# A bidirectional SSD scan's second pass: step widths moved into the exponent, both directions' decays added before one product, running sums spread by bf16 picks

## The chip, the cores and the metric

One NeuronCore of a Trainium2 chip runs the whole program. The metric is the time of one launch on the device in microseconds (us). Below, PE is TensorE, DVE is VectorE, ACT is ScalarE, POOL is GpSimd, and SP is the engine that issues most of the DMAs.

## What is computed

One encoder layer over 2560 tokens of 1024 channels (2048 of one sequence and 512 of another): RMSNorm, an input projection, neighbourhood attention and a bidirectional Mamba-2 scan side by side, an output projection, and a SwiGLU feed-forward part. The change touches the scan (8 heads of 64 channels, state of 128, 2 groups of 4 heads, chunks of 128 tokens). Cut to what matters:

```python
dt = softplus(dt_raw + dt_bias);  A = -exp(A_log)        # per direction
a_cs = cumsum(dt * A)                                    # inside a chunk of 128
Lmat = exp(where(tril, a_cs[l] - a_cs[s], -inf))
y_diag = ((C @ B.T) * Lmat) @ (x * dt)
states = B.T @ (exp(a_cs[-1] - a_cs) * x * dt)           # one per chunk
y_off  = exp(a_cs) * (C @ h_prev)                        # h_prev = h * exp(a_cs[-1]) + states
y = y_forward + y_backward + D_skip * x
g = rmsnorm_by_group(y * silu(z)) * ssm_norm_w
```

The backward direction is the same over the flipped sequence.

## The kernel before, in words

The program is a row of phases with a barrier of all engines between them: `in_proj_phase`, `attention_phase`, `ssd_phase`, `out_proj_phase`, `ffn_up_phase`, `ffn_down_phase`. Only `ssd_phase` (from L1198) is changed, and the inputs that feed it. Each engine's program is written out by hand, in order, with semaphores between engines; tiles are doubled by the chunk's parity (`par`), and loops run over 10 pairs of the 20 chunks.

Set-up (L1350 to L1389): the step widths `dt` of both directions are turned to tokens by partition, put through softplus on DVE with exponentials from ACT, and a table `tab` is filled with 16 columns each (8 heads, 2 directions) for `A_` (dt·A), `NB` (minus the running sum forward, plus the exclusive one backward), `E_` (the decay for the state's share), `DT` (dt), `CD` (a chunk's decay) and `W_` (a token's weight in the state). PE makes the running sums by products with triangles (`upper`, L1457).

First pass (to L1481), from the last chunk to the first. The helper `ahead` puts each engine one chunk ahead. PE turns x and B to tokens by partition (`turn`, L1466, L1468) and makes both directions' states (`states`, L1479). ACT copies x, B and the forward states out of PSUM (L1426, L1428, L1432). DVE copies a piece of the table (L1393), weighs x twice (`xw`, L1398) and adds the backward state `h_b` (L1406). POOL makes `h_cut`, the state times the chunk's decay (L1445). SP loads `xc` per chunk (L1326).

Second pass (L1484 to L1852), from the first chunk on. Each engine runs `step(now, after, later, before)`: it finishes chunk `now`, prepares chunk `after`, and writes out chunk `before`. In words, per step:

- PE: `across` (C times the two states, L1820, L1823), `prefixes` 0, `products` (C·B, L1779), `prefixes` 1, `diagonal` 0, `prefixes` 2, `diagonal` 1, `prefixes` 3, `turn` (L1832). A quarter q is a direction (q % 2) of a group (q // 2). `prefixes` lays a mask in PSUM by one bf16 product (L1788) and adds for each of 4 heads the running sums along the columns: the weights are one table column spread over 128 columns, the moving operand a triangle, both f32 (L1792). `diagonal` multiplies the decays by `xdt`, forward and backward into one accumulation (L1807, L1808).
- ACT: copies C·B out (`cb`, L1739), takes the exponentials of quarters 0 and 1 with the `NB` column as bias (L1744), then squares, logarithm and root of the group norm of `before` (L1751 to L1756), then quarters 2 and 3.
- DVE: `across` (L1634, L1636 from PSUM, L1639 adds the forward state `h_f`), `mix` 0 (decay times `cb`, L1625), `norm` (L1660), `mix` 2, `outputs` (L1646, L1649, L1654), `table` (copy L1616 and x·dt forward L1618), `out_turned` (L1666).
- POOL: `h_cut` (L1711), `skip` (L1715), x·dt backward (L1697), skip + off_b (L1721), `mix` 1 and 3 (L1703).
- SP: loads of B/C and z, stores of the result.

The two lines of the PE part that the change replaces:

```python
last = pe.matmul(ps_r[q % 2][:, h], tab_c[:, par, at:at + 1].broadcast_to([P, P]), upper[:, d],
                 start=False, stop=h == GH - 1)
```

## Time and profile before

| what | value |
|---|---|
| median of 3 runs | 3426.62 us (3421.67 to 3434.69) |
| the profiled execution | 3428.72 us, span of its instructions 3426.6 us |
| share of the span that PE, DVE, ACT, POOL are busy | 94%, 59%, 41%, 21% |
| granted TensorE clock, mean | 0.972 |
| scan set-up and first pass | about 1191 to 1286 us of the span |
| second pass | about 1286 to 1519 us |

The profile is one execution. A row of the timeline gives an instruction's start and duration and, in brackets, how long its engine had been idle and what released it. PE is PE's matrix products, PEld its weight loads, which overlap them; an f32 product shows as two instructions. A step of 1 in a slice's clock is 2.4 GHz.

### The profile page before, as it was taken

Reading aid. Unit: us, or ns where it says so; the run is one execution under the profiler, and the core shown is the slowest. Engines: PE = TensorE matmul, PEld = TensorE weight load, DVE = VectorE, ACT = ScalarE, POOL = GpSimd, SP = SyncE. Lnnn points to the kernel's source line nnn. Section 1 sums busy time; section 2 is a strip of 40 time slices with the busy share of each in tenths; the row PEclk is TensorE's granted clock in tenths of the full one; section 3 lists DMA queues with packets and bytes.
Section 4 is the critical chain, followed back from the end, with each engine's and each line's share of the span. In section 5 each row is a group of like instructions: output and inputs, shape, how many; then the busy total and the mean of one; then the engine's idle time right before and its main releaser. Section 6 shows DMA issues by size and latency. Waiting matters only on the chain. (4 is left out here: it accounts for less than half of the span.)

```text
span 3426.6 us, 48500 instructions
## 1 busy us (share of the span) xinstructions
PE 3205.6 (94%) x16456; PEld 2762.9 (81%) x16456; DVE 2031.9 (59%) x3070; ACT 1390.9 (41%) x2610; POOL 720.0 (21%) x683
## 2 busy tenths in 40 slices
PE   7999999996999779979979999999999998999999
PEld 6877777774777558968858999999999997887887
DVE  3446556473666578974447555755576665555655
ACT  3333434354667535542214333433343333434443
POOL 5453534412333236742220000000000000000000
PEclk9999999998999989989989999999999999999999
DMA  8686858567433032236656454745475555666776
GB/s 267 232 292 219 327 179 330 201 232 132 87 83 75 29 86 68 66 128 197 204 183 229 148 162 150 235 151 159 150 227 175 174 174 201 215 220 236 272 248 214
DMA packets 458415, 630.02 MB, mean 184 GB/s; under 512 B 133120, under 2 KB 271920, under 8 KB 453856
## 3 DMA queue, kind: packets, MB, share of 16 engines
q1 hardware_dynamic: 431808, 522.36, 48.0%
q0 software_dynamic: 23600, 100.80, 8.4%
q10 hardware_dynamic: 2880, 5.24, 0.4%
q8 instruction: 71, 1.16, 0.1%
q14 instruction: 56, 0.46, 0.0%
HBM read 451.25 MB, written 177.75 MB: 184 GB/s over the span
## 5 line engine op out<-in xcount | busy, mean ns | idle before, releaser
L65 PE MATMUL u_acc<-u_h_hi,u_w_hi 128*128 128x448 f32 (+1 forms) x1848 | 657.5, 356 | 23.9 <-DVE u_h_lo L2333 21.4
L66 PE MATMUL u_acc<-u_h_lo,u_w_hi 128*128 128x448 f32 (+1 forms) x1848 | 656.9, 355 | 0.0
L67 PE MATMUL u_acc<-u_h_hi,u_w_lo 128*128 128x448 f32 (+1 forms) x1848 | 656.8, 355 | 0.0
L65 PEld LDWEIGHTS u_acc<-u_h_hi,u_w_hi 128*128 128x128 f32 x1848 | 348.0, 188 | 44.3 <-issue 22.9
L67 PEld LDWEIGHTS u_acc<-u_h_hi,u_w_lo 128*128 128x128 f32 x1848 | 347.9, 188 | 18.5
L66 PEld LDWEIGHTS u_acc<-u_h_lo,u_w_hi 128*128 128x128 f32 x1848 | 348.0, 188 | 18.3
L2577 ACT CAST d_hi<-d_raw 128x896 fp32r<-128x896 f32 (+1 forms) x231 | 225.0, 983 | 279.4 <-PE d_acc L67 140.9
L460 DVE TENSOR_TENSOR i_w_lo<-i_raw,i_w_hi 128x2048 fp32r<-128x2048 f32 x60 | 158.0, 2633 | 295.7 <-ACT i_w_hi L332 295.7
L65 PE MATMUL d_acc<-d_hi 128*128 128x512 f32 x770 | 302.0, 392 | 17.2 <-DVE d_lo L2598 13.0
L2598 DVE TENSOR_TENSOR d_lo<-d_raw,d_hi 128x896 fp32r<-128x896 f32 (+1 forms) x231 | 252.0, 1132 | 111.1 <-ACT d_hi L2577 105.7
L66 PE MATMUL d_acc<-d_lo,d_hi 128*128 128x512 f32 x770 | 301.4, 391 | 0.0
L67 PE MATMUL d_acc<-d_hi,d_lo 128*128 128x512 f32 x770 | 301.3, 391 | 0.0
L65 PE MATMUL i_acc<-i_w_hi,i_h_hi 128*128 128x512 f32 x640 | 258.6, 404 | 15.3 <-DVE i_ev L524 15.3
L66 PE MATMUL i_acc<-i_w_lo,i_h_hi 128*128 128x512 f32 x640 | 256.7, 401 | 0.0
L67 PE MATMUL i_acc<-i_w_hi,i_h_lo 128*128 128x512 f32 x640 | 256.3, 400 | 0.0
L2276 ACT ACTIVATE u_gate<-u_gate 128x448 f32<-128x448 f32 (+1 forms) x99 | 55.8, 563 | 402.7 <-DVE u_gate L2376 206.3
L2321 DVE TENSOR_TENSOR u_w_lo<-u_w_lo,u_w_hi 128x512 fp32r<-128x512 f32 x264 | 180.6, 685 | 50.9 <-ACT u_w_hi L2261 43.5
L65 PEld LDWEIGHTS d_acc<-d_hi 128*128 128x128 f32 x770 | 145.6, 189 | 48.6 <-DVE d_lo L2598 13.3
L1164 PE MATMUL a_ps_o<-a_probT,a_v 128*64 128x128 f32 x1024 | 147.9, 283 | 34.8 <-ACT a_probT L1066 19.6
L1164 PEld LDWEIGHTS a_ps_o<-a_probT,a_v 128*64 128x64 f32 x1024 | 109.0, 138 | 85.8 <-ACT a_probT L1066 49.7
L332 ACT CAST i_w_hi<-i_raw 128x2048 fp32r<-128x2048 f32 x60 | 114.6, 1910 | 144.8 <-PE i_acc L67 140.0
L964 DVE CUSTOM_DVE_ANT_1 a_prob<-a_ps_s,a_bias 128x384 f32<-128x384 f32 (+2 forms) x160 | 93.4, 584 | 132.7 <-PE a_ps_s L1144 130.3
(256 smaller groups left out, 6411.4 us busy)
## 6 DMA issues: line engine op xcount, KB each, us to landing
u_w_lo<-w_ops SPq DMA_DIRECT2D x264, 256.0 KB, 2.9
i_raw<-w_in_dram SPq DMA_DIRECT2D x60, 1024.0 KB, 6.8
u_w_raw<-w_ffn_dram SPq DMA_DIRECT2D x198, 256.0 KB, 3.1
d_raw<-wd_ops SPq DMA_DIRECT2D x132, 256.0 KB, 5.7
d_raw<-hid_ops SPq DMA_DIRECT2D x154, 192.0 KB, 6.1
d_raw<-w_down_dram SPq DMA_DIRECT2D x99, 256.0 KB, 5.7
i_ops<-w_ffn_dram POOLq DMA_DIRECT2D x44, 512.0 KB, 6.3
w_ops<-i_ops POOLq DMA_DIRECT2D x22, 1024.0 KB, 6.9
```

The costliest lines, as they stand in the source:

```text
L65: pe.matmul(out, w_hi, x_hi, start=first, stop=False, skip_group_check=resumed)
L66: pe.matmul(out, w_hi, x_lo, start=False, stop=False, skip_group_check=resumed)
L67: return pe.matmul(out, w_lo, x_hi, start=False, stop=last, skip_group_check=resumed)
L332: act.copy(w_hi[:, par], raw[:, par]).then_inc(slot_hi_done[par], 1)
L460: dve.tensor_tensor(w_lo[:, par], raw[:, par], w_hi[:, par].bitcast(F32), ALU.subtract) \
L964: dve.tensor_tensor_reduce(prob[:, a % 4, 0:n].rearrange("p (r c) -> p r c", c=32), ps_s[a % 2][:, 0:n].rearrange("p (r c) -> p r c", c=32 ...
L1164: last = pe.matmul(ps_o[HEAD * par:HEAD * (par + 1), c], v[:, par, c * KG + FIRST[b] + j], probT[:, a % 2, j], start=j == 0, stop=j == COU ...
L2276: act.activation(gate[:, c, 0:n], gate[:, c, 0:n], ACT.Silu).then_inc(silu_done, 1)
L2321: dve.tensor_tensor(w_lo[:, n], weights(n), w_hi[:, n].bitcast(F32), ALU.subtract) \
L2577: act.copy(hi[:, r, 0:TB + w], raw[:, r, 0:TB + w]).then_inc(hi_done, 1)
L2598: dve.tensor_tensor(lo[:, r, 0:TB + w], raw[:, r, 0:TB + w], hi[:, r, 0:TB + w].bitcast(F32), ALU.subtract) \
```

## The change

It does the following.

- The bias column `NB` gets ln(dt) added (dt held at 1.2e-38 or more), so that the exponentials carry the step width. The weighed copies `xdt` (L1618 on DVE, L1697 on POOL) go, and `diagonal` takes `x_tok` itself.
- With one x for both directions, a group's two decays are added first and multiplied by `cb` once: DVE for group 0, POOL for group 1, instead of two products on each. `diagonal` then has 4 products a group instead of 8.
- The running sums are no longer made by PE for each head in the second pass. The first pass makes them once per chunk: POOL copies the chunk's `A_` columns (`a_now`), PE multiplies by the triangles (two f32 products of 16 rows), and the sums are split into three bf16 parts, high (ACT), rest (DVE), middle (ACT), low (POOL). At the end SP moves middle and low beside high, 48 rows in all. The second pass spreads a head's row by a bf16 product with constant 0/1 weights (`picks`, 48 rows).
- The second pass's table copy and the norm's two multiplies go from DVE to ACT.

The diff, cut to its core ("..." marks what is left out):

```diff
@@ first pass, set-up
+                    link(dve.tensor_scalar(na, cols(DT), SMALLEST, None, ALU.max))
+                    dve.sem_inc(dt_made, 1)
...
-                    link(dve.tensor_scalar(cols(NB, 0), half(pf, 0), -1.0, None, ALU.mult))
-                    link(dve.tensor_copy(cols(NB, 1), half(px, 1)))
+                    dve.wait_ge(log_made, 1)
+                    link(dve.scalar_tensor_tensor(cols(NB, 0), half(pf, 0), -1.0, half(na, 0), ALU.mult, ALU.add))
+                    link(dve.tensor_tensor(cols(NB, 1), half(px, 1), half(na, 1), ALU.add))
...
+                    act.activation(na, na, ACT.Ln).then_inc(log_made, 1)
@@ first pass, per chunk
+                        dve.tensor_tensor(sum_rest[:, par], ps_b[par][0:H2, KB], sums_bf[0:H2, bass.ds(c * P, P)],
+                                          ALU.subtract).then_inc(sum_rest_done[par], 1)
...
+                        act.copy(sums_bf[0:H2, bass.ds(c * P, P)], ps_b[par][0:H2, KB]).then_inc(sum_high_done[par], 1)
...
+                        act.wait_ge(sum_rest_done[par], i + 1)
+                        act.copy(sum_mid[:, bass.ds(c * P, P)], sum_rest[:, par]).then_inc(sum_mid_done[par], 1)
...
+                    def next_a(i, par, c):
+                        if not isinstance(i, int) or i > 0:
+                            pool.wait_ge(x_turned[par], i)
+                        pool.tensor_copy(a_now[:, par].unsqueeze(2), a_f_b[:, :, at(c)]).then_inc(a_ready[par], 1)
...
+                            pool.wait_ge(sum_mid_done[par], i + 1)
+                            pool.tensor_tensor(sum_low[:, bass.ds((c - par) * P, P)], sum_rest[:, par],
+                                               sum_mid[:, bass.ds((c - par) * P, P)], ALU.subtract).then_inc(sum_low_done[par], 1)
...
+                        pe.wait_ge(a_ready[par], i + 1)
+                        pe.wait_ge(sum_high_done[par], i)
+                        pe.wait_ge(sum_rest_done[par], i)
...
+                        for d in range(2):
+                            last = pe.matmul(ps_b[par][0:H2, KB], a_now[:, par, d], upper[:, d], start=d == 0, stop=d == 1)
...
+                    sp.dma_start(picks[:], pick).then_inc(picks_loaded, 16)
...
+                    sp.dma_start(sums_bf[H2:2 * H2], sum_mid[:]).then_inc(sums_moved, 16)
+                    sp.dma_start(sums_bf[2 * H2:3 * H2], sum_low[:]).then_inc(sums_moved, 16)
+                    sp.wait_ge(sums_moved, 32)
@@ second pass, DVE (POOL the same with 2, 3 and group 1)
-                    def mix(i, par, q):
...
+                        dve.wait_ge(e_done[0], c + 1)
+                        dve.wait_ge(e_done[1], c + 1)
+                        dve.tensor_tensor(decay[:, par, 0], decay[:, par, 0], decay[:, par, 1], ALU.add).then_inc(added[0], 1)
...
                     def step(now, after, later, before):
                         across(*now)
                         if after:
-                            mix(*after, 0)
-                        if before:
-                            norm(*before)
-                        if after:
-                            mix(*after, 2)
+                            mix(*after)
                         outputs(*now)
-                        if later:
-                            table(*later)
                         if before:
                             out_turned(*before)
@@ second pass, ACT
+                                act.wait_ge(cutf_done[par], i)
+                                if not isinstance(c, int) or c > 1:
+                                    act.wait_ge(off_read, c - 1)
+                                act.copy(tab_c[:, par:par + 1], tab[:, bass.ds(c, 1), 0:NTAB]).then_inc(tab_done, 1)
...
+                        act.wait_ge(rstd_done[par], i + 1)
+                        for g in range(GROUPS):
+                            c = slice(g * GW, (g + 1) * GW)
+                            act.activation(g_t[:, par, c], g_t[:, par, c], ACT.Copy, scale=rstd[:, par, g:g + 1]) \
+                               .then_inc(normed[par], 1)
@@ second pass, PE
-                            at = A_ + d * HEADS + g * GH + h
-                            last = pe.matmul(ps_r[q % 2][:, h], tab_c[:, par, at:at + 1].broadcast_to([P, P]), upper[:, d],
+                            last = pe.matmul(ps_r[q % 2][:, h], picks[:, d * HEADS + g * GH + h], sums_bf[:, bass.ds(c * P, P)],
                                              start=False, stop=h == GH - 1)
...
-                            pe.matmul(ps_y[par][:, cols], decay[:, par, 2 * g, h], xdt[:, par, 0, cols], start=True, stop=False)
-                            last = pe.matmul(ps_y[par][:, cols], decay[:, par, 2 * g + 1, h], xdt[:, par, 1, cols],
-                                             start=False, stop=True)
+                            last = pe.matmul(ps_y[par][:, cols], decay[:, par, 2 * g, h], flat2(x_tok[:, bass.ds(c, 1), cols]),
+                                             start=True, stop=True)
```

How the engines' instructions stand now. First DVE in the second pass's loop, even chunk; the rows with `s2_xdt` are the weighing, `s2_decay` the mixing. Before:

```order
L1634 TENSOR_TENSOR s2_off_f<-s2_ps_off0,s2_tab_c 128x512
L1636 TENSOR_TENSOR s2_off_b<-s2_ps_off1,s2_tab_c 128x512
L1639 ISA
L1639 TENSOR_TENSOR s_h_f<-s2_h_cut,s_s_f 128x512
L1623 REGISTER_ALU
L1625 TENSOR_TENSOR s2_decay<-s2_decay,s2_cb 128x512
L1660 TENSOR_SCALAR s2_g_t<-s2_g_t,s2_rstd 128x256 x2
L1625 TENSOR_TENSOR s2_decay<-s2_decay,s2_cb 128x512
L1646 TENSOR_TENSOR s2_off_f<-s2_ps_y0,s2_off_f 128x512
L1649 TENSOR_TENSOR s2_off_f<-s2_off_f,s2_skip 128x512
```

After, the same place:

```order
L1700 TENSOR_TENSOR s2_off_f<-s2_ps_off0,s2_tab_c 128x512
L1702 TENSOR_TENSOR s2_off_b<-s2_ps_off1,s2_tab_c 128x512
L1705 ISA
L1705 TENSOR_TENSOR s_h_f<-s2_h_cut,s_s_f 128x512
L1686 REGISTER_ALU
L1688 TENSOR_TENSOR s2_decay<-s2_decay 128x512
L1691 TENSOR_TENSOR s2_decay<-s2_decay,s2_cb 128x512
L1712 TENSOR_TENSOR s2_off_f<-s2_ps_y0,s2_off_f 128x512
L1715 TENSOR_TENSOR s2_off_f<-s2_off_f,s2_skip 128x512
```

The norm has left the queue, and what follows the add is one product. The norm and the table copy stand on ACT now, in the loop's odd chunk:

```order
L1782 COPY s2_tab_c<-s_tab 128x72
L1783 REGISTER_ALU
L1784 COPY s2_cb<-s2_ps_cb 128x256
L1790 ACTIVATE s2_decay<-s2_ps_r0,s2_tab_c 128x128 x4
L1790 ACTIVATE s2_decay<-s2_ps_r1,s2_tab_c 128x128 x4
L1797 ACTIVATE s2_junk,s2_ss<-s2_g_t 128x256 x2
L1800 ACTIVATE s2_ss_ln<-s2_ss,s_eps 128x2
L1802 ACTIVATE s2_rstd<-s2_ss_ln 128x2
L1806 ACTIVATE s2_g_t<-s2_g_t,s2_rstd 128x256 x2
```

Quarters 2 and 3 of the exponentials come behind L1806. On POOL, in the first pass's loop, a small copy (`a_now`, for the chunk after the next) stands ahead of each h_cut and a subtraction of 16 rows behind it, where h_cut stood alone:

```order
L1506 TENSOR_TENSOR s1_h_cut<-s_h_b,s1_tab_c 128x512
L1509 ISA
L1509 TENSOR_TENSOR s1_sum_low<-s1_sum_rest,s1_sum_mid 16x128
L1491 ISA
L1491 COPY s1_a_now<-s1_a_f_b 128x32
L1506 ISA
L1506 TENSOR_TENSOR s1_h_cut<-s_h_b,s1_tab_c 128x512
```

The next chunk's `a_now` copy is thus queued behind this chunk's subtraction.

## Rows read from the trace of the kernel before

**Rows 1.** The page's busy time, share of the span, instructions, by engine.

```profile
PE 3205.6 (94%) x16456; PEld 2762.9 (81%) x16456; DVE 2031.9 (59%) x3070; ACT 1390.9 (41%) x2610; POOL 720.0 (21%) x683
```

**Rows 2.** Stretches: length, busy time by engine, PE clock, DMA share, GB/s.

```profile
1222.00:1286.00 64.00, 55.74 (x280) 45.28 (x280) 54.54 (x80) 28.95 (x60) 28.28 (x20) 0.94 0.39 111
1286.00:1298.00 12.00, 8.42 (x45) 7.76 (x46) 3.98 (x6) 5.80 (x17) 2.81 (x2) 0.72 0.27 89
...
1384.90:1406.95 22.05, 21.13 (x170) 20.05 (x169) 20.76 (x27) 12.02 (x47) 16.59 (x12) 1.00 0.25 71
```

**Rows 3.** Timeline, PE in one chunk of the second pass: start, us, what.

```profile
1398.34 0.10 PEld L1788 LDWEIGHTS s_ps_r<-s_masks,s_ident_bf 128*128 128x128 bf16 x1 [1.32 <-DVE s_tab_c L1616]
...
1399.35 0.53 PEld L1779 LDWEIGHTS s_ps_cb<-s_bc 128*128 128x128 f32 x4
1399.80 0.10 PEld L1788 LDWEIGHTS s_ps_r<-s_masks,s_ident_bf 128*128 128x128 bf16 x1
...
1399.91 0.38 PE L1788 MATMUL s_ps_r<-s_masks,s_ident_bf 128*128 128x512 bf16 x1
...
1400.12 1.05 PE L1792 MATMUL s_ps_r<-s_upper,s_tab_c 128*128 128x128 f32 x8
...
1400.91 0.30 PEld L1807 LDWEIGHTS s_ps_y<-s_xdt,s_decay 128*128 128x128 f32 x2
...
1402.64 0.15 PEld L1788 LDWEIGHTS s_ps_r<-s_masks,s_ident_bf 128*128 128x128 bf16 x1
...
1406.58 0.47 PEld L1832 LDWEIGHTS s_ps_t<-s_ident,s_g_t 128*128 128x128 f32 x4
1407.02 0.73 PEld L1820 LDWEIGHTS s_ps_off<-s_h_f,s_bc 128*128 128x128 f32 x4
...
1408.64 0.10 PEld L1788 LDWEIGHTS s_ps_r<-s_masks,s_ident_bf 128*128 128x128 bf16 x1
```

**Rows 4.** Timeline, DVE and POOL in the second pass.

```profile
1385.92 0.19 DVE L1616 COPY s_tab_c<-s_tab 128x72 f32 x1
...
1389.69 1.49 POOL L1697 TENSOR_TENSOR s_xdt<-s_x_tok,s_tab_c 128x512 f32<-128x512 f32 x1
...
1390.20 1.52 DVE L1625 TENSOR_TENSOR s_decay<-s_decay,s_cb 128x512 f32<-128x512 f32 x1
...
1394.19 0.68 DVE L1625 TENSOR_TENSOR s_decay<-s_decay,s_cb 128x512 f32<-128x512 f32 x1
...
1408.02 0.19 DVE L1616 COPY s_tab_c<-s_tab 128x72 f32 x1
```

**Rows 5.** Timeline, products and ACT; group norm of the last chunk.

```profile
1498.28 0.53 PEld L1779 LDWEIGHTS s_ps_cb<-s_bc 128*128 128x128 f32 x4
...
1499.09 0.37 ACT L1739 COPY s_cb<-s_ps_cb 128x256 f32<-128x256 f32 x1 [2.63 <-PE s_ps_cb L1779]
...
1499.36 2.18 ACT L1744 ACTIVATE s_decay<-s_ps_r,s_tab_c 128x128 f32<-128x128 f32 x8
...
1514.75 0.42 ACT L1751 ACTIVATE s_junk<-s_g_t 128x256 f32<-128x256 f32 x1 [5.79 <-DVE s_g_t L1654]
...
1516.02 0.20 ACT L1756 ACTIVATE s_rstd<-s_ss_ln 128x2 f32<-128x2 f32 x1
```

**Rows 6.** Timeline, DVE and POOL in the first pass.

```profile
1248.38 2.14 DVE L1398 TENSOR_TENSOR s_xw<-s_x_tok,s_tab_c 128x512 f32<-128x512 f32 x2
1248.41 1.56 POOL L1445 TENSOR_TENSOR s_h_cut<-s_h_b,s_tab_c 128x512 f32<-128x512 f32 x1 [1.41 <-DVE s_h_b L1406]
...
1251.35 2.14 DVE L1398 TENSOR_TENSOR s_xw<-s_x_tok,s_tab_c 128x512 f32<-128x512 f32 x2
```

**Rows 7.** POOL groups by form to 1300 us: count, busy us, mean ns.

```profile
L906 POOL TENSOR_TENSOR a_prob<-a_prob,a_inv 128x512 f32<-128x512 f32 x32 | 33.3, 1042 | 79.1 <-DVE a_inv L979 79.1
...
L906 POOL TENSOR_TENSOR a_prob<-a_prob,a_inv 128x256 f32<-128x256 f32 x16 | 9.8, 614 | 57.0 <-DVE a_inv L979 57.0
```

**Rows 8.** DMA issues of the scan: count, KB each, median us to landing.

```profile
s_bc<-xcT SPq DMA_DIRECT2D x20, 256.0 KB, 3.2
```

More of the change, by code:

```diff
@@ L1264, in ssd_phase @@
             h_cut = sb1("h_cut", [P, 2, D_SSM])
+            a_f_b = sb1("a_f_b", [P, 2, NCH, H2])
+            a_now = sb1("a_now", [P, 2, 2, H2])
+            sum_rest = sb1("sum_rest", [H2, 2, P])
+            sum_mid = sb1("sum_mid", [H2, T], BF16)
+            sum_low = sb1("sum_low", [H2, T], BF16)
             ps_x = [ps1(f"ps_x{i}", [P, KX, P]) for i in range(2)]
@@ L1532, in ssd_phase @@
             e_done = four("e_done")
-            m_done = four("m_done")
+            added = two("added")
+            m_done = two("m_done")
             cb_out = two("cb_out")
@@ L1654, in outputs @@
                         dve.tensor_tensor(g_t[:, par], off_f[:, par], z_t[:, par], ALU.mult).then_inc(gated[par], 1)
-                    def norm(i, par):
-                        dve.wait_ge(rstd_done[par], i + 1)
-                        for g in range(GROUPS):
-                            c = slice(g * GW, (g + 1) * GW)
-                            dve.tensor_scalar(g_t[:, par, c], g_t[:, par, c], rstd[:, par, g:g + 1], None, ALU.mult) \
-                               .then_inc(normed[par], 1)
                     def out_turned(i, par):
@@ L1722, in step @@
                         if after:
[L1723 to L1728 removed]
+                            mix(*after)
+                    mix(0, 0)
                     steps(pool, step)
```

113 lines of the change are left out of this document (64 added, 49 removed).

## Prediction

> **What bounds the kernel now.** I read the page first: TensorE (PE) is busy 94% of the span [rows 1], but that is a mean over phases, and the change touches one phase only, the two scan passes, 327 us of 3427. So I went to the stretches [rows 2]: the first pass takes 64 us for 20 chunks, and in a pair of chunks of the second pass (22.05 us) PE is busy for 21.1 and DVE for 20.8, while ACT has 12.0 and POOL 16.6. Two engines are full there. Then the timeline of PE's weight loads in one chunk [rows 3], where the distance between starts is what a piece really costs. I name them: across (A, four f32 products of 256 columns) 1.62 us, a prefix block (r, one bf16 mask product and four f32 products) 1.11, the C·B products (P) 0.45, a half of the diagonal (D, 8 f32 products) 1.73, the turn (T) 0.44. One chunk is A + 4r + P + 2D + T = 10.4 us. Once a pair PE also sits 1.32 us for DVE's table copy (first of rows 3). The copy recurs after 1408.02 - 1385.92 = 22.10 us [rows 4]: 11.05 us a chunk, and DVE sets it as much as PE.
>
> What DVE spends is partly not its own. Its mix product started at 1390.20 and took 1.52 us, though it is 0.68 where POOL is idle (1394.19); POOL's weighing of x had started at 1389.69 [rows 4]. In the first pass two DVE products of about that length take 2.14 when POOL's h_cut starts 0.03 us behind the first: 0.65, then POOL's piece of some 0.9, then the second 0.6, which is the end of both rows [rows 6]. So operations of DVE with both inputs in SBUF and operations of POOL take turns, about 0.6 us and 1.0 us each.
>
> **Second pass: PE.** The prefix block loses its f32 products for bf16 ones. The mask product, 512 columns in bf16, is followed by the next after 0.21 us [rows 3], so 128 columns are 0.055 by its rate; the bounds are 0.055 and the 0.11 at which f32 passes follow each other (8 in 1.00). I take 0.06: r = 0.11 + 0.22 + 4 x 0.06 = 0.5 with some rounding up (at 0.11 it is 0.66). The Trainium skill ("TensorE: Matmul & The Clock Gate", LDWEIGHTS) puts a weight load at its columns over 1.2 in ns, 107 for 128 columns however few its rows; by that picks would follow at the 0.11 bound, r would be 0.66 and the ring below 8.1 instead of 7.9, still under what I take for the chunk. D has half the products: 0.87, and with a register instruction ahead of each at most 1.3. One chunk is then 1.62 + 4 x 0.5 + 0.45 + 2 x 0.87 + 0.44 = 6.3 us, 7.7 with both upper bounds. PE stops being the bound.
>
> **Second pass: the ring over ACT and PE.** ACT takes over the table copy and the two normalising multiplies, in its in-order queue between quarters 0, 1 and 2, 3 of the decays. PE's turn waits for the multiplies, PE's across, prefix 0 and products stand behind the turn, ACT's cb copy waits for the products, the exponentials stand behind that, the group norm behind them. Once round, per chunk: T 0.49 with its wait, A 1.62, r0 0.5 [rows 3]; products to cb copy 1499.09 - 1498.28 = 0.81, cb to the first exponential 0.27, eight exponentials 2.18 less the last one's tail, 2.0, squares to rstd 1.47 [rows 5]; two multiplies of 256 columns 0.7 (0.42 is such a square, the second overlaps). With one wait of 0.05 that is **7.9 us**. Before, the multiplies were DVE's and PE's queue hid all of this. The moved table copy (0.19 on DVE, about 0.2 on ACT) runs while ACT waits for the products; if that cover goes it costs 0.2 a chunk. The exponent now carries ln dt; that is free there.
>
> **Second pass: the port pair.** DVE loses the table copy, the dt product and the norm; its two mix products become an add and a product. With two SBUF inputs remain h_f, add, product, + skip, gate: 5 x 0.6 = 3.0 us. POOL loses the weighing and keeps five: h_cut, skip, + off_b, add, product: 5 x 1.0 = 5.0. Together 8.0 us, and DVE's other four (from PSUM, 0.6 each, 2.4) run beside POOL. That is just above the ring's 7.9. The turns do not pack: POOL's add waits for quarter 3, and while DVE reads y from PSUM (0.6) POOL is often out of work. I take **8.4 us** a chunk; the floor is 7.9 (ring), the ceiling 9.2 (8.0 + the 0.6 of y + 0.6 of waits between turns). The Trainium skill ("SBUF — State Buffer", Who interferes with whom) states this as an exclusive lock held for a whole instruction. If it were a sharing of bandwidth instead, the ring alone would decide, 7.9; rows 4 and 6 speak for turns.
>
> Saving: 19 chunk periods x (11.05 - 8.4) = **-50.4 us**. The head of the second pass runs at the lower clock (0.72 in 1286 to 1298 [rows 2]) and its first prefixes shorten by about 1 us each: -2 (0 to -3).
>
> **First pass.** DVE is full: period 1251.35 - 1248.38 = 2.97 us [rows 6]. Each chunk gains a subtraction of 128 columns (DVE; between the 0.19 of a 72-column copy [rows 4] and 0.65 of 512 columns: 0.25), two ACT copies of 16 rows (ACT has 1.3 us free), two f32 products on PE (0.43; PE has 0.5 free), and on POOL sum_low and the copy a_now. POOL's 256 columns take 0.61 and its 512 take 1.04 [rows 7], so by a straight line 0.40 and 0.24. The DVE term alone gives 3.22. But POOL is in order, and a ring closes over two chunks: h_b ends, h_cut (0.3 wait, 1.5), sum_low behind DVE's second weighing (to +3.4 us), a_now (+3.65), the two products and their end (+4.4), ACT's copy of x (+5.1), both weighings (+7.2), the subtraction, h_b: 7.3 us for two, 3.65 each. I take 3.64: 19 x 0.67 = **+12.7 us**. Bounds 3.22 (+4.8) and 3.9 (+17.7, each small POOL operation 0.25 dearer over two chunks). Small POOL operations are in no row of this phase, so the ring could be wrong by more than that.
>
> At the end SP moves two 16-row tensors inside SBUF and waits for them, with every engine behind it at the block's end: between an issue alone, 0.4, and that with the landing of a bc load of 256 KB, 3.2 [rows 8], so 3.6. These move 80 KB each; nearer the upper row, I take **+3.0**. The load of picks is issued while the last chunks run and is hidden; if not, at most its own landing, 3. The set-up chain gains a max and a Ln, both under the running-sum products (3.6 us of PE there), and POOL's parts copy, hidden behind DVE's table work: +0.5 for two operations that become two-input ones.
>
> **Sum** against the profiled execution, 3428.7 us (its span is 3426.6): -50.4 - 2 + 12.7 + 3.0 + 0.5 = -36.2, 3392.5. The median of the runs shown is 2.1 lower, so I forecast **3390 us**, 1.1% less. All later phases start earlier and are otherwise unchanged.
>
> **Rivals.**
> *The ring alone decides* (turns pack perfectly, first pass pays only DVE's 0.25): 19 x (11.05 - 7.9) = 59.9; -59.9 - 2 + 4.8 + 3.5 = -53.6, 3373. For it: POOL and DVE already interleave well in rows 4. Against: 8.0 of turns is more than 7.9. Chance 0.20.
> *DVE and POOL do not pack*, 9.2 a chunk: 19 x 1.85 = 35.2; -35.2 - 2 + 12.7 + 3.5 = -21, 3406. For it: POOL would be in work 5.5 of 9.2, and both engines wait for each other three times a chunk (h_cut, off_b, skip). Chance 0.22.
> *The first pass loses more*: the POOL ring at 4.5 us, +29 instead of +12.7, with 8.4 behind it: 3406 too. It means that small POOL operations cost twice the straight line. Chance 0.05.
> *Slower: the clock falls.* PE goes from 21.1 busy of 22.05 to 6.3 of 8.4 a chunk, with a wait of a microsecond or more in each. Rows 2 show the granted clock at 0.72 where PE had stood idle for the bc load, and 1.2 GHz is its lower level. If the whole second pass ran there, PE's 6.3 would be 12.6 us a chunk: 19 x 1.55 = +29, and with the first pass +46: 3472. It costs more than it saves once more than about six tenths of the pass are at the lower level. The Trainium skill's page on TensorE and its clock gate says that idle stretches bring the clock down, which speaks against this change. Against it: the first pass, with PE waiting in every chunk (busy 55.7 of 64), had 0.94 granted including its start [rows 2]. Chance 0.03.
>
> **Numbers.** Forecast (8.2 to 8.7 a chunk) 0.50; the five cases are 0.50, 0.20, 0.22, 0.05, 0.03. A measurement of this kernel can tell about 0.5%, 17 us, from no change. Faster by more needs under 3409.5: the forecast, the ring alone, most of the other two: 0.87. Within 0.5%: 0.09. Slower 0.04. The range holds the first three cases and some of the bounds: 3370 to 3411. The forecast's own is 3383 to 3399.
>
> **What would show it.** Right: a chunk of the second pass recurs every 8.2 to 8.7 us; PE's gap stands ahead of the products or the diagonal, not ahead of prefix 0 for a DVE copy; bf16 picks at about 0.06 us; ACT idle only for the cb copy; DVE's add or product over 1 us when POOL runs. First pass: x copies every 3.6 us, PE's a_now products released by POOL, and about 3 us between the last h_b and the first bc load. Wrong: a period at or under 8.0 (no turns), POOL idle over 3 us a chunk (the ring is longer than I have it), a granted clock under 0.9 in the second pass, or a first-pass period above 4.

## The result, and the profile after

The changed kernel takes 3406.48 us (median of 11 executions, 3391.67 to 3423.13) against 3426.62 of the kernel before (median of the 11 timed beside it): a ratio of 0.9938, with an interval of 0.9917 to 0.9959, so 14 to 28 us less. The forecast was 3390. The profiled execution took 3394.09 us, 34.6 less than the profiled one of before. So there are two questions: whether the 34.6 came from where they were forecast, and why the median has only 20 of them.

The page's busy line of the changed kernel, against [rows 1]:

```profile
PE 3157.7 (93%) x15896; PEld 2674.9 (79%) x15896; DVE 1968.5 (58%) x3011; ACT 1410.6 (42%) x2711; POOL 703.6 (21%) x706
```

It says little: PE does 48 us less, and the span is 34 shorter. The stretches say more. First pass, the gap between the passes, and 30 us of the second pass (length; busy time of PE, PEld, DVE, ACT, POOL; granted clock, DMA share, GB/s), against [rows 2]:

```profile
1217.00:1294.00 77.00, 68.70 (x360) 49.74 (x358) 43.34 (x99) 35.57 (x100) 42.76 (x59) 0.97 0.33 94
1294.00:1306.00 12.00, 4.56 (x20) 2.29 (x20) 0.20 (x1) 4.21 (x12) 0.00 (x0) 0.62 0.38 102
1380.00:1410.00 30.00, 25.95 (x187) 18.96 (x186) 29.09 (x34) 24.92 (x95) 25.01 (x19) 1.00 0.29 86
```

PE is no longer full in the second pass; DVE is in work for 97% of it. The chunk recurs every 8.47 and 8.55 us by turns, where it took 11.05. These rows, of one chunk, are the ring that the forecast described, from one group norm to the next (ACT and PE, in order of time):

```profile
1399.24 0.48 ACT L1797 ACTIVATE s_junk<-s_g_t 128x256 f32<-128x256 f32 x1
...
1400.80 0.91 ACT L1806 ACTIVATE s_g_t<-s_g_t,s_rstd 128x256 f32<-128x256 f32 x2
...
1401.83 0.42 PEld L1876 LDWEIGHTS s_ps_t<-s_ident,s_g_t 128*128 128x128 f32 x4 [1.28 <-issue]
1402.22 0.73 PEld L1864 LDWEIGHTS s_ps_off<-s_h_f,s_bc 128*128 128x128 f32 x4
...
1403.84 0.10 PEld L1837 LDWEIGHTS s_ps_r<-s_masks,s_ident_bf 128*128 128x128 bf16 x1
1404.36 0.22 PEld L1840 LDWEIGHTS s_ps_r<-s_sums_bf,s_picks 48*128 48x128 bf16 x4 [0.42 <-issue]
1404.69 0.52 PEld L1830 LDWEIGHTS s_ps_cb<-s_bc 128*128 128x128 f32 x4
...
1405.44 0.37 ACT L1784 COPY s_cb<-s_ps_cb 128x256 f32<-128x256 f32 x1 [1.53 <-PE s_ps_cb L1830]
1405.70 2.18 ACT L1790 ACTIVATE s_decay<-s_ps_r,s_tab_c 128x128 f32<-128x128 f32 x8
...
1407.71 0.48 ACT L1797 ACTIVATE s_junk<-s_g_t 128x256 f32<-128x256 f32 x1
```

Squares to multiplies 1.56, to PE's turn 1.03, turn 0.39, across 1.62, prefix 0 0.85, products to the cb copy 0.75, to the exponentials 0.26, these 2.01: 8.47 us, the period itself. ACT's idle 1.53 ahead of the cb copy is no reserve, for what it waits for stands behind its own multiplies. The picks' products follow one another after 0.056 us, as forecast, but the block of prefix 0 is 0.85 long and the others are 0.65 to 0.74, not 0.5. The idle 0.42 ("issue") is that of the weight loads between the mask's and the first pick's; part of it is the mask product itself, as the products show:

```profile
1404.05 0.38 PE L1837 MATMUL s_ps_r<-s_masks,s_ident_bf 128*128 128x512 bf16 x1
1404.37 0.39 PE L1840 MATMUL s_ps_r<-s_sums_bf,s_picks 48*128 x4
```

The picks start 0.32 us behind the mask product, where an f32 product of before stood 0.21 behind it [rows 3]: 0.1 us is new there.

The other candidate, the turns of DVE and POOL, in the same chunk:

```profile
1400.83 1.59 POOL L1765 TENSOR_TENSOR s_skip<-s_skip,s_off_b 128x512 f32<-128x512 f32 x1
1401.22 1.75 DVE L1688 TENSOR_TENSOR s_decay<-s_decay 128x512 f32<-128x512 f32 x1
1403.01 0.69 DVE L1691 TENSOR_TENSOR s_decay<-s_decay,s_cb 128x512 f32<-128x512 f32 x1
```

DVE's addition takes 1.75 behind POOL's, and the product after it, with POOL idle, 0.69. Turns are there as forecast; both candidates lie near 8.5, and only runs can tell which decides.

The first pass went from 2.97 to 3.75 us a chunk (forecast 3.64). Its rows, for [rows 6]:

```profile
1244.38 0.58 ACT L1464 COPY s_x_tok<-s_ps_x 128x512 f32 x1 [1.34 <-PE s_ps_b L1541]
1245.16 1.29 DVE L1433 TENSOR_TENSOR s_xw<-s_x_tok,s_tab_c 128x512 f32<-128x512 f32 x2 [1.66 <-issue]
1245.28 0.29 ACT L1471 CAST s_sum_mid<-s_sum_rest 16x128 f32 x1
1245.76 0.98 POOL L1509 TENSOR_TENSOR s_sum_low<-s_sum_rest,s_sum_mid 16x128 f32 x1 [1.02 <-ACT s_sum_mid L1471]
1246.69 0.20 POOL L1491 COPY s_a_now<-s_a_f_b 128x32 f32 x1
1246.95 0.44 PE L1539 MATMUL s_ps_b<-s_ident,s_xc 128*128 128x128 f32 x2 [0.49 <-POOL s_a_now L1491]
1247.31 0.61 PE L1541 MATMUL s_ps_b<-s_upper,s_a_now 128*16 128x128 f32 x4
...
1248.06 0.59 ACT L1464 COPY s_x_tok<-s_ps_x 128x512 f32 x1 [1.33 <-PE s_ps_b L1541]
```

PE waits for POOL's a_now, which stands behind sum_low, which waits for ACT's sum_mid, which follows ACT's copy of x, which follows PE: a ring of one chunk, not over two as forecast. DVE now idles (1.66 us ahead of the weighing). At the end of the pass (SP's queue, and the first issue of the next block):

```profile
1293.59 0.64 SPq L1351 DMA_DIRECT2D s_sums_bf<-s_sum_mid  x1
1294.28 0.57 SPq L1352 DMA_DIRECT2D s_sums_bf<-s_sum_low  x1
1297.33 0.39 SPq L1653 DMA_DIRECT2D s_bc<-xcT  x1
```

The last h_b is done by 1293.98; the next block opens 3.35 us later (0.3 before the change). The move is the cause: in the kernel that has the sums in place, below, the next block opens 0.3 us behind it again.

### The profile page after: what moved, and what is told of

Read it like the earlier page. It is cut to its first block and busy times, and to the rows that moved or that the text cites. A ratio compares the mean times of both kernels' runs of the same rounds, so it can differ in the third digit from the quotient of the medians.

```text
span 3392.3 us, 47727 instructions
## 1 busy us (share of the span) xinstructions
PE 3157.7 (93%) x15896; PEld 2674.9 (79%) x15896; DVE 1968.5 (58%) x3011; ACT 1410.6 (42%) x2711; POOL 703.6 (21%) x706
## 5 line engine op out<-in xcount | busy, mean ns | idle before, releaser
L65 PEld LDWEIGHTS u_acc<-u_h_hi,u_w_hi 128*128 128x128 f32 x1848 | 347.7, 188 | 45.2 <-DVE u_w_lo L2366 22.8
L460 DVE TENSOR_TENSOR i_w_lo<-i_raw,i_w_hi 128x2048 fp32r<-128x2048 f32 x60 | 155.3, 2589 | 305.6 <-ACT i_w_hi L332 305.6
L1164 PE MATMUL a_ps_o<-a_probT,a_v 128*64 128x128 f32 x1024 | 148.0, 283 | 34.2 <-ACT a_probT L1066 19.6
L2306 ACT CAST u_w_hi<-u_w_lo 128x512 fp32r<-128x512 f32 x264 | 152.7, 616 | 43.5 <-DMA u_w_lo<-w_ops 43.5
```

Source lines behind the costliest of these rows:

```text
L65: pe.matmul(out, w_hi, x_hi, start=first, stop=False, skip_group_check=resumed)
L460: dve.tensor_tensor(w_lo[:, par], raw[:, par], w_hi[:, par].bitcast(F32), ALU.subtract) \
L1164: last = pe.matmul(ps_o[HEAD * par:HEAD * (par + 1), c], v[:, par, c * KG + FIRST[b] + j], probT[:, a % 2, j], start=j == 0, stop=j == COU ...
L2306: act.copy(w_hi[:, n], weights(n)).then_inc(w_hi_done, 1)
```

## Experiments

Every kernel was timed beside the kernel before on one chip, and its stretches were taken from one profiled execution: start of the scan phase to the first h_b (37.5 us in nearly all), first to last h_b ("pass 1"), last h_b to first gT ("between"), first to last gT ("pass 2"), and all to the first product of out_proj ("scan").

| kernel | ratio to before (interval) | pass 1 | between | pass 2 | scan | clock, 1380 to 1410 |
|---|---|---|---|---|---|---|
| before | 1 | 55.9 | 36.1 | 196.7 | 340.6 | 1.00 |
| changed | 0.9938 (0.9917 to 0.9959) | 69.3 | 34.6 | 156.2 | 311.8 | 1.00 |
| changed, again | 0.9939 (0.991 to 0.9968) | 69.1 | 34.8 | 179.2 | 334.6 | 0.84 |
| a_now early | 0.99 (0.9875 to 0.9925) | 62.3 | 34.9 | 156.4 | 305.1 | 1.00 |
| no picks | 0.9873 (0.9848 to 0.9898) | 56.1 | 34.4 | 159.7 | 302.2 | 1.00 |
| decays not added | 0.9939 (0.9915 to 0.9963) | 69.3 | 35.2 | 162.7 | 318.4 | 1.00 |
| ACT longer | 1.0038 (1.0017 to 1.006) | 69.3 | 33.5 | 205.7 | 360.5 | 0.83 |
| norm on DVE | 1.0003 (0.9977 to 1.0028) | 69.3 | 37.4 | 186.6 | 344.5 | 0.85 |
| skip on PE | 0.9937 (0.991 to 0.9964) | 69.2 | 34.2 | 162.8 | 317.4 | 1.00 |
| sums in place | 0.9915 (0.9886 to 0.9944) | 68.5 | 31.6 | 163.6 | 315.3 | 0.89 |
| PE filled | 0.9911 (0.988 to 0.9943) | 69.0 | 34.8 | 155.3 | 310.8 | 1.00 |
| turn later | 0.991 (0.9876 to 0.9945) | 69.2 | 37.9 | 154.1 | 312.5 | 0.94 |
| combined | 0.9853 (0.9822 to 0.9883) | 68.8 | 34.7 | 147.6 | 301.9 | 1.00 |
| combined, sums moved | 0.9895 (0.9871 to 0.9918) | 62.3 | 39.3 | 148.0 | 301.1 | 1.00 |

One thing outside the change must be taken off before spans are compared: FFN-up takes 1090 to 1092 us in some profiled executions and 1105 to 1107 in others (both in these kernels), and the scan phase starts between 1180 and 1192. The stretches don't have that difference of 15 us; the medians do.

**The changed kernel again.**

> The changed kernel once more, unchanged, as the yardstick for the three beside it. Its profiled execution had gained 34.6 us, its median only some 20. If the profile is typical of the passes and the medians differ by the clock elsewhere, both scan passes show again 3.7 and 8.5 us a chunk and the median is again 15 to 25 us under the kernel before. If the profiled execution was a lucky one in the passes, one of the two periods comes out longer here.

Median 3406.98, 17.7 under the kernel before. The profiled execution took 3427.12 us, and its second pass is the one that differs: 10.2 us a chunk. 30 us of that pass:

```profile
1380.00:1410.00 30.00, 26.75 (x157) 19.25 (x156) 20.61 (x27) 20.27 (x78) 18.07 (x15) 0.84 0.27 79
```

Three pieces of one chunk (length, PEld busy, granted clock, DMA share, GB/s):

```profile
1408.00:1410.00 2.00, 1.52 (x9) 0.68 0.00 0
1410.00:1412.00 2.00, 1.48 (x5) 0.50 0.15 47
1412.00:1414.00 2.00, 1.05 (x14) 0.97 0.80 231
```

And its timeline, of PE with ACT's cb copy:

```profile
1409.97 1.62 PEld L1867 LDWEIGHTS s_ps_off<-s_h_b,s_bc 128*128 128x128 f32 x4
1411.68 0.15 PEld L1837 LDWEIGHTS s_ps_r<-s_masks,s_ident_bf 128*128 128x128 bf16 x1
...
1413.50 0.37 ACT L1784 COPY s_cb<-s_ps_cb 128x256 f32<-128x256 f32 x1 [3.21 <-PE s_ps_cb L1830]
...
1418.30 0.42 PEld L1876 LDWEIGHTS s_ps_t<-s_ident,s_g_t 128*128 128x128 f32 x4 [1.21 <-ACT s_g_t L1806]
```

In every chunk PE stands for 1.21 to 1.28 us ahead of the turn, and the across products behind it run at 0.50, the lower level of 1.2 GHz: half of across takes 1.62 instead of 0.84, all of it 3.08 instead of 1.62. The turn between the wait and across takes what it took in the other execution. Across and prefix 0 stand in the ring, so it grows from 8.47 to 10.2, and DVE drops from 97% to 69%. Both periods of the first pass are the same in the two executions; the second pass is not. In the other execution the wait is as long (1.28) and the clock stays at 1.00 from about 1330 to 1460, up to the last steps, so the wait alone does not decide it; what does, no row here shows. The Trainium skill ("TensorE: Matmul & The Clock Gate", HAM oscillation — how this bites in real kernels) describes such a cycle, in which a wait for a DMA in each tile, a longer one than here, makes the next tile start at the low clock. This execution has the same cycle, chunk for chunk, with its shorter wait; the first one, with the same wait and the upper level, doesn't.

The unprofiled executions show the two courses too, in the mean granted clock of the whole program. Of the changed kernel's 21 executions ten have 0.962 to 0.967 and eleven 0.969 to 0.973. The medians of the two groups are 3416.2 and 3395.2 us: 21 apart, near the 22.8 by which the two profiled scans differ. The kernel before has 0.970 or more in all 73 executions whose clock is on record. So the changed kernel gains some 30 us in one course and some 10 in the other, and its median lies between. (The executions of either course are spread by FFN-up's 15 us besides.)

**a_now early.** Its edit, on POOL:

```
-   next_a(...)                 # ahead of h_cut, behind the last chunk's sum_low
    h_cut ...
+   if not last: next_a(i + 1, par, c - 2 - par)
    sum_low ...
```

> The step products of a chunk (a_now) are copied by POOL ahead of the third part of the sums (sum_low), not behind it. Theory: the first pass recurs every 3.7 us because x copy, high, rest, mid, sum_low, a_now and PE's turn close a ring of one chunk; with a_now ahead it opens, the period falls to 3.1 to 3.3 us (DVE's own work) and the program is 8 to 11 us shorter than the changed kernel. Rival: the ring runs over the state (h_b, h_cut, sum_low, next h_cut) or over ACT alone; then the period stays at 3.6 to 3.7 us and the time within 3 us. The second pass stays at 8.5 us in both.

x copies of ACT in this kernel, and POOL's copy:

```profile
1243.78 0.67 POOL L1491 COPY s_a_now<-s_a_f_b 128x32 f32 x1
...
1245.62 0.59 ACT L1464 COPY s_x_tok<-s_ps_x 128x512 f32 x1 [0.93 <-PE s_ps_b L1540]
...
1249.03 0.59 ACT L1464 COPY s_x_tok<-s_ps_x 128x512 f32 x1 [0.93 <-PE s_ps_b L1540]
```

The period is 3.27 and 3.42 by turns, a little over the 3.1 to 3.3 expected; pass 1 is 7.0 us shorter and the scan 6.7, where 8 to 11 were expected. The ring through sum_low and a_now was the bound, and 0.41 of the 0.78 us a chunk that the first pass had lost were this order of two instructions. DVE's own work is not the next bound. From one h_b (1241.70) to the one two chunks on (1248.39) pass 6.69 us, the two periods, over h_cut, a_now, PE's products, ACT's copy of x (1245.62), the weighings and the subtraction: the ring that the forecast described, without sum_low in it.

**No picks.** The prefix blocks go back to f32, the sums to nothing:

```
-   last = pe.matmul(ps_r[q % 2][:, h], picks[:, ...], sums_bf[:, bass.ds(c * P, P)], ...)
+   last = pe.matmul(ps_r[q % 2][:, h], tab_c[:, par, at:at + 1].broadcast_to([P, P]), upper[:, d], ...)
    (rest, sum_mid, sum_low, a_now and the move of the first pass out)
```

> Only the sums by bf16 picks are undone: the prefix blocks of the second pass take the four f32 products of the kernel before again, the first pass makes no sums and the move at its end is gone; ln dt in the exponent, the added decays and the work moved to ACT stay. Theory (port turns of DVE and POOL set 8.5 us, PE has room): PE goes from 6.3 to 8.7 us a chunk and is just the bound, period 8.8 to 9.2; that is +6 to +13 us, against 13 + 3.3 us given back in the first pass and at its end: 3 to 10 us shorter than the changed kernel, so the picks alone would have been a loss. Rival (the ring over ACT and PE is near 8): prefix 0 stands in the ring and waits for ACT's table copy besides, so the period is 9.5 or more, +19, and the whole is 2 us or more longer than the changed kernel.

```profile
1380.00:1410.00 30.00, 30.00 (x236) 28.35 (x235) 29.19 (x31) 22.84 (x88) 23.79 (x18) 1.00 0.27 79
```

PE is full, the period 8.89 as expected, pass 1 back at 56.1: the scan takes 302.2 against 311.8 us. Its median is 40 us under the kernel before, where the changed kernel's is 18 under on the same chip. So the picks, the largest part of the change, lose: they give 0.38 us a chunk of the second pass (3.5 us from first to last gT), cost 13 in the first pass, and leave PE the wait behind which its clock falls. With a_now early the picks still lose, but only 2.9 us by the scans (305.1 against 302.2). (The 3 us of the move are not seen in "between": from the first C·B load to the first across pass 7.7 us with f32 prefixes and 5.6 with picks.) The rival, 9.5 us or more, is out.

**Decays not added.**

```
-   decay0 = decay0 + decay1;  decay0 = decay0 * cb         (DVE; POOL alike)
+   decay0 = decay0 * cb;      decay1 = decay1 * cb
-   8 products per chunk, decay[:, par, 2 * g, h] by x_tok
+   16 products, decay[:, par, 2 * g + d, h] by x_tok, start=d == 0, stop=d == 1
```

> Only the addition ahead of one product is undone: DVE and POOL multiply both directions' decays by C.B, one after the other (two products where the changed kernel has a sum and a product), and PE takes 16 f32 products for the diagonal instead of 8, 1.74 us more a chunk on its measured 7.2. Theory (ring, port and PE all near 8.5, the clock down only where PE idles over a microsecond a chunk): PE becomes the bound at 8.9 to 9.2 us and does not idle, so the clock stays at 1.00 and the median is within 6 us of the changed kernel's, because what PE loses the clock gives back. Rival (the clock falls in this pass for another reason): 9.0 at best and 10.5 or more in the slow executions, median 8 us or more above the changed kernel's.

```profile
1380.00:1410.00 30.00, 30.00 (x227) 23.39 (x226) 27.89 (x31) 21.53 (x82) 24.04 (x18) 1.00 0.28 80
```

8.98 us a chunk, all of it at 1.00, the scan 318.4, between the two executions of the changed kernel (311.8 and 334.6), and the median the same as the changed kernel's to 0.01%. None of its twelve executions has a mean clock under 0.970, so the rival is out: what the addition saves PE, the clock takes back in part of the executions.

**ACT longer, and the norm on DVE.**

```
    ACT: + activation(junk, g_t, Copy, scale=rstd) twice, ahead of the two multiplies
    DVE: + tensor_scalar(g_t, g_t, rstd, mult) twice behind the product of decays; - ACT's two
```

> ACT makes the two normalising multiplies of a chunk twice, the first time into a scratch tile (0.9 us more on ACT, ahead of PE's turn). Theory (the ring norm, turn, across, prefix 0, products, cb copy, four times two exponentials, rstd, norm has no slack at 8.5 us): the period goes to 9.3 or 9.4 us. Rival (turns of DVE and POOL at their port set 8.5 and ACT has the 1.5 us to spare that it waits for the products): 8.5 to 8.7 us, at most 4 us in all.

> The two normalising multiplies go back from ACT to DVE, behind DVE's product of decays. Theory (ring without slack): the ring loses ACT's 0.9 and gains DVE's 0.7 and a wait for DVE's place in its own order, 8.5 to 9.0 us. Rival (DVE and POOL set the period): DVE, 97% full at 8.5, gains 0.7, so 9.1 to 9.3 us, +12 to +15 us. Where PE has to wait longer for the multiplies, the granted clock of the pass is 0.84 or less.

With 0.9 more on ACT the period is 11.4 on average (10.8 to 11.7), 1.2 over the changed kernel's chunk in its low course. The norm on DVE gives 10.3, dearer than either sum said, since both sums left the clock out. In both, all twelve executions have a mean clock of 0.966 or less. So a longer wait on PE (2.0 us ahead of the turn with ACT longer, 0.9 and 2.6 by turns with the norm on DVE) put every execution into the low course. Neither run had a chunk at 1.00 throughout, so the port rival's 8.7 failed as a number, but neither run separates ring and port at the upper level. In these two kernels the addition to PE's wait cost more than itself (2.9 us a chunk for 0.9), and both lose the whole gain of the change.

**Skip on PE.**

```
-   POOL: skip = x_tok * D;  skip = skip + off_b
+   PE:   ps_y += x_tok by d_diag[:, head], 8 products ahead of the wait for m_done
-   DVE:  off_f + skip
+   DVE:  off_f + off_b
```

> POOL's weighing of x by D and its addition of off_b are taken out of the second pass: PE makes x times D by eight more f32 products against diagonal weights (ahead of the wait for the decays), and DVE adds off_b where it added the skip. DVE's operations are as many as before, POOL has three instead of five, PE goes from 6.3 to 7.2 us a chunk. Theory (turns at the shared port are the bound, 5 x 0.6 + 5 x 1.0): two turns of 1.0 go, and the period falls from 8.5 to 7.3 to 7.7 us, 15 to 23 us in all. Rival (the ring over ACT and PE, 7.9): the period stays between 8.0 and 8.8, and the gain is under 8 us. PE the bound: over 8.8.

```profile
1380.00:1410.00 30.00, 30.00 (x232) 23.89 (x230) 19.10 (x30) 22.77 (x87) 13.58 (x12) 1.00 0.34 97
```

This was a miss: I had put the eight products at 0.9 us; they are 0.87 for each four, 1.74, and PE became the bound at 8.98. DVE fell from 97% to 64% busy and POOL from 83% to 45%, but with PE the bound this doesn't tell what the period would be with fewer turns.

**PE filled.** Two unused products of 256 columns ahead of the turn's wait:

```
+   for _ in range(2): pe.matmul(ps_cb[:, 2:4], ident[:], upper[:, 0:2], start=True, stop=True)
    pe.wait_ge(normed[par], 2 * i + 2)
```

> PE runs two f32 products of 256 columns into unused columns of a PSUM bank (0.8 us) ahead of its wait for the normalised chunk in every step of the second pass; nothing uses them. Theory (the wait of 1.2 us there is what takes the clock down in some executions of the changed kernel, and that costs 1.7 us a chunk): the granted clock stays at 1.00 behind the head, the period is 8.5 us in every execution, and the median comes to 30 us or more under the kernel before, with the slow ones of 3425 us gone. Rival (the clock falls for another reason, or the wait that is left is enough): executions still spread from 3391 to 3427 us, median 20 us under the kernel before.

```profile
1380.00:1410.00 30.00, 29.91 (x198) 21.61 (x197) 28.91 (x33) 24.92 (x97) 24.07 (x18) 1.00 0.36 103
```

8.52 us at 1.00 from 1320 on. Its six executions lie between 3392 and 3407 us, where the changed kernel has eight of 21 above 3410; the median is 31.8 under the kernel before. The intervals of the two ratios overlap, so the median's gain by itself is likely, not shown. The clocks say more: none of the six is in the low course, against ten of 21 of the changed kernel, from which it differs by the two products alone; by luck that would be some 2% (an estimate, 11/21 to the sixth power). The other kernels fit. Four more have no idle time of PE's weight loads over 0.5 us in 1380 to 1410 (no picks, decays not added, skip on PE, combined with the sums moved), and the combined one has 0.85: none of their 40 executions has a mean clock of 0.967 or less. All six with a wait of some 1 us or more in each chunk have such executions: the changed kernel 10 of 21, a_now early 3 of 6, ACT longer 12 of 12, norm on DVE 12 of 12, sums in place 2 of 9, turn later 3 of 6. The kernel before waits 1.32 us [rows 3] too, but only once in two chunks, and has none.

**Turn later.** PE's turn, DVE's gT and the store move one step on:

```
    step(now=c):  across(c)
+                 turn(c - 2)
                  prefixes, products, diagonal ...
-                 turn(c - 1)
```

> PE's turn of a chunk, DVE's copy out of it and the store come one step later, behind the across products of the next chunk, so that PE no longer waits for ACT's multiplies ahead of across. Theory (ring without slack): across and the turn's wait drop out of the ring, the period falls to the port's sum, 7.9 to 8.3 us, 5 to 11 us in the pass, and PE's wait ahead of the turn goes, so the clock stays at 1.00 and the median gains some 12 us more. Rival (port turns alone decide): the period stays at 8.5 us and only the clock is mended.

PE's wait is now elsewhere, ahead of across, for DVE's h_f. Two chunks that follow one another, and the clock of two pieces:

```profile
1351.71 0.73 PEld L1868 LDWEIGHTS s_ps_off<-s_h_f,s_bc 128*128 128x128 f32 x4 [1.06 <-DVE s_h_f L1708]
1360.00 1.35 PEld L1868 LDWEIGHTS s_ps_off<-s_h_f,s_bc 128*128 128x128 f32 x4 [1.05 <-DVE s_h_f L1708]
```

```profile
1360.00:1390.00 30.00, 28.55 (x165) 21.11 (x166) 26.36 (x33) 21.47 (x83) 21.95 (x16) 0.83 0.32 96
1390.00:1420.00 30.00, 27.20 (x197) 20.05 (x195) 25.97 (x30) 24.98 (x97) 24.52 (x19) 1.00 0.27 79
```

Where the clock holds, the period is 8.29, with across and the wait out of the ring. So the ring was the bound at 8.47 to 8.55, and the turns of DVE and POOL, as it seems, the next one, 0.2 below: DVE is in work for 29.4 of 30 us there, and PE and ACT are not. The clock was not mended: behind a wait of 1.05 us at another place it falls too, now and then.

**Sums in place; the combined kernel; the combined one with the sums moved.**

```
    rows 0, 64, 96 of one tile: high in all 112 rows, mid over 64.., low over 96..; no DMA
    pool.tensor_copy(a_now[:, par, :, :, 0:H2], a_f_b[...].broadcast_to([P, 2, 4, H2]))
    combined: + turn(c - 2), + 2 unused products ahead of across's wait, + 4 at the pass's start
    combined, sums moved: the same without the rows in place
```

> The three parts of the running sums are made in place in rows 0, 64 and 96 of one tile (PE makes the sums in four row groups at once, ACT and DVE run their same operations over more rows, DVE makes the low part instead of POOL), the picks are spread over the same rows, and the two DMAs at the end of the first pass with their wait are gone; the a_now copy is also early, as in the run before. Theory (the wait is 3.3 us of pure standstill): the distance from the last h_b to the first gT falls from 34.7 to 31.5 us, the first pass stays at the 62.3 us of the early copy, and the whole is 10 us shorter than the changed kernel. Rival (the load of bc or of the picks ends just as late, so the standstill only changes its name): 34 us or more.

> All that helped, together: a_now early, the sums' parts in place without a move at the end, the turn one step later, and PE kept in work (two unused f32 products ahead of its wait for h_f in each chunk, four at the start of the second pass). Theory: first pass 62, 31 between the passes, second pass 8.29 us a chunk at clock 1.00 in every execution (152 us from first to last gT): the scan phase takes 295 to 298 us against 311.8 of the changed kernel, and the median is 45 us or more under the kernel before. Rival (the products in PE's wait delay across, or the clock falls all the same): 8.6 us a chunk or more, scan phase over 303 us.

> The combined kernel without the sums in place: a_now early, the turn one step later and PE kept in work, but three parts of 16 rows with the move by DMA at the end of the first pass, as in the changed kernel. Sum of the stretches measured apart: set-up 37.5, first pass 62.3 instead of the combined kernel's 68.8 (POOL's copy of a_now is 0.2 us again, not 0.75), 38 from the last h_b to the first gT (3.3 more than in the combined kernel), second pass 147.6, 14.2 behind it: 299.6 us for the scan phase against 301.9, so the two medians agree within what can be told. If POOL's wider copy is not what made the combined kernel's first pass long, the first pass is 68 us here too.

The move's 3.3 us are gone where the sums are in place: "between" is 31.6 against 34.9 with a_now early alone. But pass 1 is 6 us longer, so that the scan, expected 10 us shorter than the changed kernel's, is 3.5 longer in a profile whose second pass has a clock of 0.89 in part. In the first pass, with the sums in place, DVE makes the low part ahead of each h_b, and POOL's copy of a_now is wider:

```profile
1244.96 0.75 POOL L1491 COPY s_a_now<-s_a_f_b 128x128 f32 x1
1246.49 0.29 DVE L1436 TENSOR_TENSOR s_sums_bf<-s_sum_rest,s_sums_bf 16x128 f32 x1
```

Both stand in the ring over two chunks, which takes 7.41 us from h_b (1243.01) to h_b instead of 6.69. From the subtraction of the rest to h_b it takes 0.43 more, the weighings and what waits for their end 0.27 more (2.14 us beside POOL's h_cut instead of 1.87), and the wider copy only 0.08 (0.75 instead of 0.67). So DVE's new subtraction is the larger part, not the copy.

Something else changed that was not meant to. PE's block of prefix 0 in the combined kernel, with picks of 112 rows instead of 48, by its weight loads and then by its first products:

```profile
1392.59 0.10 PEld L1838 LDWEIGHTS s_ps_r<-s_masks,s_ident_bf 128*128 128x128 bf16 x1
1392.69 0.43 PEld L1841 LDWEIGHTS s_ps_r<-s_sums_bf,s_picks 112*128 112x128 bf16 x4
1393.08 0.53 PEld L1831 LDWEIGHTS s_ps_cb<-s_bc 128*128 128x128 f32 x4
...
1392.69 0.38 PE L1838 MATMUL s_ps_r<-s_masks,s_ident_bf 128*128 128x512 bf16 x1
1392.91 0.39 PE L1841 MATMUL s_ps_r<-s_sums_bf,s_picks 112*128 x4
```

The first pick is loaded beside the mask product and starts 0.22 us behind it instead of 0.32. The picks' products follow one another after 0.055 us with either number of rows, and one pick's weight load takes 0.09 to 0.10 with either. The block takes 0.49 us, against 0.74 at the same place, behind the turn, in the kernel with the sums moved. The kernel with the sums in place alone has the same blocks (0.60 behind across, against 0.85), and its chunks at the upper level take 8.0 to 8.4 us. A ring 0.25 shorter would be at 8.2 to 8.3, where the turns are too, so this run doesn't separate the two.

Without the sums in place the first pass is short again, which fits but takes out the copy and DVE's subtraction together: pass 1 is 62.3 in the last kernel, with copies of 0.67 us and not the 0.2 expected, between 39.3, the scan 301.1, where 299.6 were added up beforehand. The combined kernel's second pass:

```profile
1380.00:1410.00 30.00, 27.65 (x200) 22.56 (x200) 29.26 (x35) 24.91 (x95) 25.02 (x19) 1.00 0.36 105
```

8.25 us at 1.00, with DVE in work for 98% of it; with the sums moved, and so with the narrow picks, it is 8.30. PE's blocks hardly count there, which speaks for the turns as the bound. The combined kernel takes 3378.87 us (median of 6), 48 under the kernel before and faster than the changed kernel beyond both intervals; the scan's stretches came to 301.9, 4 to 7 us over what was expected, because pass 1 is 68.8 instead of 62 ("between" and pass 2 together are 182.3, where 183 were expected). Between it, its sibling and the kernel without picks (302.2, the simplest of the three) the stretches show no difference worth naming.

## Why the prediction was right, and where it was wrong

**The number** fell into the range (3370 to 3411) and the side was right, but the profiled execution agreed with the sum, -36.2 against -34.6, partly by chance: 5.4 us of it lie ahead of the scan phase, which the change does not touch. The scan itself gave 28.8.

**The second pass's 8.4 us** was right where the clock holds (8.51). It was reached by the wrong one of two near candidates. The ring was forecast at 7.9; the step that failed is r = 0.5 for the block of picks (0.85 in the ring) and 0.7 for the multiplies (1.03 to the turn). With these, and a turn 0.1 shorter, it is 8.47 to within 0.03. Part of the miss in r is the sum itself: 0.11 + 0.22 + 4 x 0.06 is 0.57, not 0.5, and 0.77 at the 0.11 bound, not 0.66. The rest is what 48 rows cost over 112, 0.25 a block, which no row of before could show. The sign given for the ring failed as well: PE's gap stands ahead of the turn, which waits for the multiplies, and not ahead of the products or the diagonal. The turns were put at 8.0 to 9.2 with 8.4 taken; out of the ring's shadow they give 8.25 to 8.29. Nor did r move PE alone: a chunk of PE is 7.2 us, not 6.3.

**19 periods of saving** overstated it. From the first bc issue to the last gT the saving is 231.8 - 186.8 = 45.0 us, against 52.4 forecast (with the head): the last two steps are short in either kernel (10.7 us before, 8.8 after), and one early step took 11.47.

**The first pass**: +13.4 against +12.7, the right size. The ring named was not the one that bound the pass, a loop over two chunks through h_b; the one that did closes in one chunk through ACT's sum_mid, sum_low and a_now. Both have POOL's order in them, so the expectation "PE's products released by POOL" held. The ring named became the bound once the two instructions were swapped. The straight line's prices for small POOL operations, 0.40 and 0.24, hold where DVE is not in the way (sum_low 0.42 in the last chunk, a_now 0.20); beside DVE's weighing sum_low takes 0.98. That the turns apply to POOL's small operations too was in no term.

**The move at the end**: 3.35 less the 0.3 of before, 3.0 forecast. Set-up: nothing instead of 0.5.

**The clock** was the rival with 0.03, and it deserved far more: ten of 21 executions took the low course. It was dismissed because the first pass, with short waits, had 0.94. Its price was wrong too: not all of PE's work doubles, only across (+1.46) and, in part, prefix 0 (+0.22), +1.7 us a chunk, +23 in the pass. That takes the scan from 311.8 to 334.6 in such an execution, so that 6.0 of its gain of 28.8 us are left, and the median gain is some 20. The change would lose as a whole not at six tenths of the pass at the rival's price but at 0.45 (36.2 of 19 x 4.2), for the first pass's loss comes on top. The two medians of the changed kernel, 3406.5 and 3407.0, lie where the rival "don't pack" had put them, but for another reason: that the median fell near the middle of the range is luck. The Trainium skill ("TensorE: Matmul & The Clock Gate"), quoted in the prediction as speaking against the change, had the direction right: the second profiled execution (0.84) agrees with it, the first (1.00) doesn't.

## What to carry to other kernels

When an engine that was full becomes one that waits, look at its clock and not only at its work: here the added decays bought nothing in the median and the picks less than nothing, and part of the reason is that a PE without such waits had the upper level behind the start of the pass in every profile. Close every ring with the durations of the new form, and look for the in-order neighbour (here a small copy behind a small subtraction) that closes it. And undo each part of a change by itself: of this one, the part with the most lines was a loss, in part for the shape of its weights (48 rows between products of 128, 0.25 us a block).

## What the runs showed that was not expected

- The same program has two courses in the second pass, 8.5 and 10.2 us a chunk, with the same wait of 1.2 us on PE, and can change from one to the other within the pass (turn later: 0.83, then 1.00; sums in place waits 1.5 us a chunk and does so too). What decides is open.
- The block with narrow picks is the longer one: 0.65 to 0.85 us with 48 rows against 0.40 to 0.60 with 112 at the same places. The picks themselves follow one another after 0.055 us in both; the narrow ones start 0.1 us later behind the mask product (0.31 against 0.22), and the product behind the last of them 0.09 later (0.146 against 0.055). By the Trainium skill ("TensorEngine Tiling (Array Packing)", Tiling Modes, Key Properties) a change of the tiling mode drains the array, and 48 rows fit its 64-row mode, which 112 and 128 don't; the rows agree with it, but none shows which mode a product runs in. The Trainium skill's figure for weight loads, quoted in the prediction ("TensorE: Matmul & The Clock Gate", LDWEIGHTS: 107 ns for 128 columns however few the rows), is near the single loads here, 94 ns with 48 rows and 98 with 112, hardly different. The loads overlap, though, so that it doesn't set the distance of the picks.
- POOL's subtraction of 16 rows by 128 columns takes 0.87 to 0.98 us beside DVE's weighing, nearly as long as a 512-column operation of POOL with DVE out of the way (1.04), and 0.42 in the last chunk, where no weighing runs beside it.
